# Placing the matmul operands of a three-block transformer at other bytes of SBUF

## The reference, cut to what matters

```python
def swiglu(h, w13, w2):
    a, b = jnp.split(h @ w13, 2, axis=-1)
    return (jax.nn.silu(a) * b) @ w2
...
        h = modulate(x, norm_g[l, 0], sh1, sc1)
        x = x + 0.5 * g1[:, None] * swiglu(h, ff_w13[l, 0], ff_w2[l, 0])
...
def moe_swiglu(h, w_router, w_gate, w_up, w_down):
...
    def expert_block(args):
        xb, e = args
        return swiglu_2(xb, w_gate[e], w_up[e], w_down[e])
```

## Time and profile before

| | |
|---|---|
| three runs | 3090.5 us median, 3087.42 to 3091.05 |
| span of the profiled execution | 3083.6 us |
| PE | busy 2999.6 us (97%), 20659 matmuls |
| DVE, ACT | busy 76% and 56% of the span |
| granted TensorE clock | 0.9 of full speed or more in each of the page's 40 slices |
| DMA | 240 GB/s in the mean |

### The profile page before, as it was taken

One profiled execution on the slowest core, in us unless ns is written; L12 is line 12 of the kernel. 1 busy time (PEld: TensorE's weight loads), 2 busy tenths in 40 slices (PEclk: granted clock), 3 DMA queues, 4 the chain that ended last, 5 costly groups with the idle time before them and its releaser, 6 DMA issues.

```text
span 3083.6 us, 48420 instructions
## 1 busy us (share of the span) xinstructions
PE 2999.6 (97%) x20659; PEld 2751.1 (89%) x20659; DVE 2343.1 (76%) x2704; ACT 1725.0 (56%) x1982; POOL 73.7 (2%) x143
## 2 busy tenths in 40 slices
PE   9999999999989999899989999999999999999999
PEld 8999899999979998899987888888888888899999
DVE  6887788888657566665777898898898898766675
ACT  5435443534535445444655777777777777555553
POOL 0110001010000000000000000000000000000000
PEclk9999999999999999999999999999999999999999
DMA  8785468587513543255415998998999899533353
GB/s 335 283 317 195 163 245 302 212 308 258 199 69 142 215 162 138 76 192 191 148 64 209 364 358 334 365 355 333 365 356 366 333 359 366 213 124 137 123 201 114
DMA packets 112381, 739.27 MB, mean 240 GB/s; under 512 B 12480, under 2 KB 12480, under 8 KB 32160
## 3 DMA queue, kind: packets, MB, share of 16 engines
q1 hardware_dynamic: 92304, 662.77, 57.3%
q0 software_dynamic: 19856, 73.34, 6.8%
HBM read 735.01 MB, written 1.05 MB: 239 GB/s over the span
## 4 chain that ended last, share of the span: by engine, by line
PE 86%; DVE 9%; ACT 3%; issue 1%; DMA 0%; SPq 0%; DVEq 0%; ACTq 0%
PE ps L560 65%; PE ps L559 19%; PE ps L569 2%; DVE wlo L2983 2%; ACT whi L1986 2%; DVE AF L2962 1%; DVE att L2971 1%; DVE T L2953 1%; DVE hl L2953 1%; DVE gf L2965 0%; ACT cv L1971 0%; DMA ring<-in_r 0%; DVE cv L2962 0%; DVE T L2962 0%; DVE AR L2962 0%
## 5 line engine op out<-in xcount | busy, mean ns | idle before, releaser
L2983 DVE TENSOR_TENSOR wlo<-ring,whi 128x2048 fp32r<-128x2048 f32 x620 | 1416.3, 2290 | 399.0 <-ACT whi L1986 398.3
L1986 ACT ACTIVATE whi<-ring 128x2048 fp32r<-128x2048 f32 x620 | 1184.4, 1914 | 310.6 <-issue 199.0
L560 PE MATMUL ps<-whi,AR 128*128 128x512 f32 (+1 forms) x2884 | 910.7, 392 | 0.3 <-DVE AF L2953 0.3
L560 PE MATMUL ps<-hh,whi 128*128 128x256 f32 x2272 | 641.8, 282 | 0.4 <-DVE hl L2953 0.4
L560 PEld LDWEIGHTS ps<-whi,AR 128*128 128x128 f32 x2884 | 535.5, 188 | 115.3 <-DVE AF L2953 0.7
L560 PE MATMUL ps<-hl,whi 128*128 128x256 f32 x2272 | 634.4, 279 | 0.0
L560 PE MATMUL ps<-hh,wlo 128*128 128x256 f32 x2272 | 634.3, 279 | 0.0
L560 PE MATMUL ps<-wlo,AR 128*128 128x512 f32 (+1 forms) x1442 | 557.4, 387 | 0.0
L560 PEld LDWEIGHTS ps<-hh,whi 128*128 128x128 f32 x2272 | 426.2, 188 | 5.8 <-issue 1.5
L560 PEld LDWEIGHTS ps<-hl,whi 128*128 128x128 f32 x2272 | 426.1, 188 | 1.2 <-issue 1.0
L560 PEld LDWEIGHTS ps<-hh,wlo 128*128 128x128 f32 x2272 | 425.9, 187 | 0.3
(11 more groups left out here) (275 smaller groups left out, 3481.6 us busy)
## 6 DMA issues: line engine op xcount, KB each, us to landing
ring<-in_w SPq DMA_DIRECT2D x620, 1024.0 KB, 4.9
rring<-in_r POOLq DMA_DIRECT2D x135, 512.0 KB, 5.0
first<-in_r SPq DMA_DIRECT2D x8, 512.0 KB, 18.4
ring<-in_r SPq DMA_DIRECT2D x4, 512.0 KB, 8.6
rring<-in_r SPq DMA_DIRECT2D x3, 512.0 KB, 17.4
AF<-in_mem SPq DMA_DIRECT2D x1, 1024.0 KB, 8.2
X<-in_x SPq DMA_DIRECT2D x1, 1024.0 KB, 16.2
AF<-in_cst POOLq DMA_DIRECT2D x1, 1024.0 KB, 5.3
```

The costliest lines, as they stand in the source:

```text
L560: return self.e.matmul(out, l, r, start=start, stop=stop)
L1986: self.e.activation(N.whi[:, c % HB, :], N.ring[:, c % RING, :], ACT.Copy).then_inc(N.sem["hi"], 1)
L2983: self.e.tensor_tensor(N.wlo[:, c % HB, :], N.ring[:, c % RING, :], N.whi[:, c % HB, :].bitcast(F32), ALU.subtract).then_inc(N.sem["lo"], 1)
```

## The change

No instruction is added, taken away or moved: on every engine the two programs have the same rows in the same order with the same waits. What changes is the byte at which some operands begin. The tiles `ca` and `gain` change places around `hh` and `hl`, a tile `gap` of 160 bytes that nothing uses stands ahead of `AR`, `AF` and `T`, and the unshifted early halves get a place of their own with a pitch of 256 numbers (`vh` and `vl`, picked by a new function `early_halves`).

The table has the first byte of each operand in its partition, as what is left of it over a multiple of 256. It follows from the sizes of the tiles: `X` begins at byte 16512, `ring` and the tiles up to `misci` stay where they were, and `AR` begins at byte 179488 before and 179648 now.

| operand | before | now |
|---|---|---|
| `whi`, `wlo` (every 128 or 512 columns of them) | 128 | 128 |
| `hh`, `hl`, each row | 160 | 64 |
| `f_gh`, `f_gl`, each row | 160 | 64 |
| unshifted early halves | 32, 64, 96, ... 0 for k = 0 to 7 | 64 in each row |
| shifted early halves | 32, 64, 96, ... 0 for k = 0 to 7 | 192, 224, 0, ... 160 |
| experts' `e_zeh`, `e_zel`, `e_gh`, `e_gl` | 32 | 192 |
| other tiles in `AR`, `AF` and `T` | 32 and others | 160 bytes on |

```diff
         self.X = sb("X", [P, 8, S])
-        self.ca = sb("ca", [P, 8])
+        self.gain = sb("gain", [P, 2, 3, 8])
         self.hh = sb("hh", [P, 8, S], F32R)
         self.hl = sb("hl", [P, 8, S], F32R)
-        self.gain = sb("gain", [P, 2, 3, 8])
+        self.ca = sb("ca", [P, 8])
         self.g12 = sb("g12", [P, 8])
...
         self.misci = sb("misci", [1, 8], I32)
+        self.gap = sb("gap", [P, 40])
         with nc.sbuf_tensor("AR", [P, 12288], F32R) as a:
             self.AR = a
...
         ar.n = 3840
         self.uh, self.ul = ar.take(8, UP), ar.take(8, UP)
         assert ar.n <= self.AF.shape[1] - 8 * S
+        ar = Arena(self.AR)
+        ar.n = 3872
+        self.vh, self.vl = ar.take(8, S), ar.take(8, S)
+        assert ar.n <= self.AF.shape[1] - 8 * S
...
+def early_halves(net, key):
+
+    return (net.uh, net.ul) if EARLY[key][0] == "mod" else (net.vh, net.vl)
...
         n = S + 2 if EARLY[h][0] == "mod" else S
+        uh, ul = early_halves(N, h)
...
-                    t = self.mm3(b[j][:, 0:n], whi[:, o:o + P], wlo[:, o:o + P], N.uh[:, k, 0:n], N.ul[:, k, 0:n],
+                    t = self.mm3(b[j][:, 0:n], whi[:, o:o + P], wlo[:, o:o + P], uh[:, k, 0:n], ul[:, k, 0:n],
                                  k == 0, k == 7)
```

More of the change, by code:

```diff
@@ L2095, in early @@
         gain, shift = gain_of(N, which)
+        uh, _ = early_halves(N, key)
         if self.loaded:
@@ L2104, in early @@
                 self.ready_x(j)
-                self.act(N.uh[:, j, 0:S], N.X[:, j, :], ACT.Copy, (key, "uhi", j), scale=gain[:, j:j + 1])
+                self.act(uh[:, j, 0:S], N.X[:, j, :], ACT.Copy, (key, "uhi", j), scale=gain[:, j:j + 1])
             if k == 0 and shift is not None:
-                self.act(N.uh[:, :, S:S + 2], shift.unsqueeze(2).to_broadcast([P, 8, 2]), ACT.Copy, (key, "ush"))
+                self.act(uh[:, :, S:S + 2], shift.unsqueeze(2).to_broadcast([P, 8, 2]), ACT.Copy, (key, "ush"))
             self.act(N.T[:, k:k + 2, :], N.X[:, k:k + 2, :], ACT.Square, (key, "sq", k), (key, "sq", k + 1))
@@ L3147, in early_after @@
         gain, shift = gain_of(N, EARLY[key])
+        uh, ul = early_halves(N, key)
         def rest(k):
@@ L3151, in rest @@
                 self.wait_ge("act", (key, "ush"))
-                self.tt(N.ul[:, :, S:S + 2], shift.unsqueeze(2).to_broadcast([P, 8, 2]), N.uh[:, :, S:S + 2].bitcast(F32),
+                self.tt(ul[:, :, S:S + 2], shift.unsqueeze(2).to_broadcast([P, 8, 2]), uh[:, :, S:S + 2].bitcast(F32),
                         ALU.subtract)
             self.wait_ge("act", (key, "uhi", k))
-            self.stt(N.ul[:, k, 0:S], N.X[:, k, :], gain[:, k:k + 1], N.uh[:, k, 0:S].bitcast(F32), ALU.mult, ALU.subtract,
+            self.stt(ul[:, k, 0:S], N.X[:, k, :], gain[:, k:k + 1], uh[:, k, 0:S].bitcast(F32), ALU.mult, ALU.subtract,
                      (key, "un", k))
```

## The result

The changed kernel takes 3067.1 us (median of four runs, 3060.5 to 3071.7) where the kernel before takes 3089.0 in the same comparison: a ratio of 0.9928, interval [0.9913, 0.9944]. It is faster by 22 us, 0.7%, where 75 us were forecast; the time lies 0.1 us past the end of the range.

A forecast was written before the change was run, and what follows sets the result against it. PE's matmul pace was taken as the bound; gains of 31.5 + 40.4 + 3 = 75 us off the 3083.6 us span give 3008.6, and 6.9 us from span to median gives 3015.5 us, range 2994 to 3067.

The forecast's parts named there:

- The rest: Unshifted early halves and some 670 further 256-column matmuls were to gain 3 us together; other engines' work was to stay unchanged.
- split x and gated halves: 11,664 matmuls of 256 columns, moved from byte 160 to 64, were to go from 116.7 to 113.7 ns: 31.5 us.
- The worst bound that I worked out: Smallest gain for the split x and gated halves: 115 ns per matmul, 19.8 us.
- The factor of 0.9: Share of the 256-column matmuls' 35.0 us gain taken to reach the end of the span, giving 31.5 us.
- the place makes no difference: Reading of memory products at byte 32 (120 ns) and 258-column halves at bytes 64 and 96 (120.8 ns and 1.44 us per 12).
- experts: 4038 matmuls of 512 columns, stationary moved from byte 32 to 192, were to go from 233.3 to 223.3 ns: 40.4 us.
- The first rival: The experts don't respond, perhaps because the moving operand's own byte, 64, counts: 3056 us, chance 0.20.
- it could fetch earlier: In the experts, the weights' queue waits 794.6 of 900 us for a freed buffer, so weights could keep up at 381 GB/s.
- the fourth rival: DMA or DVE holds PE up in the experts, and half of the 40.4 us stays: 3036 us, chance 0.10.
- Slower: Runs of `hh` and the gated halves settle at 120 ns and lose 35 us: 3125 us, chance 0.06.
- no change: The nine matmuls at 113.3 ns owe their pace to rows ahead; runs return to 116.7: 3090.5 us, chance 0.06.
- the forecast's own range: Times expected if the experts' matmuls take 220 to 226.7 ns: 2994 to 3040 us; the forecast's chance was 0.58.

The follow-up runs named there:

- experiment 3: Not the reference's work: 72 matmul streams alone, one per pair of start bytes, 256 or 512 columns; 113.3 to 120.0 ns per matmul at 256 columns, 226.7 to 234.4 at 512.
- experiment 4: Not the reference's work: 48 streams alone of 96 matmuls of 256 columns at bytes 64 and 128, 40 with an odd 49th matmul; 113.3 or 117.8 ns per matmul.
- experiments 5 to 7: The changed kernel with experts' stationary operands at byte 128 (3047.8 us), at byte 64 (3053.4 us), and at byte 128 plus 31 extra 254-column matmuls (3055.1 us).
- experiment 1: The changed kernel with the experts' stationary operands put back to byte 32, all else kept: 3065.5 us, ratio 0.9923 to the kernel before.
- experiment 5: The changed kernel with the experts' stationary operands at byte 128, the byte of their moving weights, instead of 192: 3047.8 us, ratio 0.9867 to the kernel before.
- experiment 8: The kernel of experiment 5 with only the first half of each expert weight chunk's columns fetched: 3047.4 us, ratio 0.9874 to the kernel before.

## Why the prediction was right and wrong

**Right: the place changes the pace of a matmul, and PE's pace is the time.** DVE, ACT and the 258-column halves (120.3 ns in the mean before, 120.2 now) stayed as they were. "The rest", 3 us, came out near its size: the unshifted early halves went from 117.7 to 115.1 ns (1.0 us), the matmuls with a weight as the moving operand from 118.9 to 116.7 (1.5 us). The Trainium skill, "SBUF — State Buffer", section "Who interferes with whom", calls PE's two read ports independent; by that rule experiment 3 would show one pace for all pairs, and it shows 113.3 to 120.0 ns with nothing else running.

**Wrong, step "split x and gated halves": "PE settles ... on a pace" and "a run of 48 matmuls or more now keeps it".** The nine matmuls of the earlier trace rows showed one of two stable states at that difference of bytes. A run does keep its state, but about a third of the matmuls are in the other one, at 117.8 ns. The term was 113.7 ns and 31.5 us; measured are 114.85 ns and 22.4 us of PE's work. The worst bound that I worked out, 115 ns, was the better guess. The factor of 0.9 is not what failed: 22 us of time for 25 us of PE's work (22.4 and 2.5 of the rest) do not speak against it.

The trace of the kernel before already had the sign. Its memory products, all at bytes 32 and 128, ran 15 matmuls in 1.80 us from 19 us on the earlier trace rows, but 12 us later in 33.37 - 31.61 = 1.76, 117.3 ns each, like k = 0 of the earlier trace rows at the same bytes:

```profile
31.61 0.28 PE L560 MATMUL ps<-AR,wlo 128*128 128x256 f32 x1
...
33.37 0.28 PE L560 MATMUL ps<-AR,wlo 128*128 128x256 f32 x1
```

Two paces at one pair of bytes, 120.0 and 117.3, were read as "the place makes no difference". Experiments 3 and 4 show both states of the pair 64 and 128 without any other work; what chooses between them inside the kernel is open: the second block's feed-forward had the better state in all eight profiled executions with operands at 64 and 128, the last one in three of eight (experiments 5 to 7).

**Wrong, step "experts": "so again the moving operand lies 64 bytes below the stationary one".** The good difference at 256 columns is not the good one at 512. There it is 0, which at 256 columns is among the worst (120.0 ns, and k = 3 of the earlier trace rows). The step carried a price from one shape to another with no row of the second; 40.4 us became nothing, as experiment 1 shows. The first rival had the outcome, with a wrong reason: it is not the moving operand's own byte, since 128 and 192 give 113.3 ns with 256 columns.

**Wrong, though it decided nothing: "it could fetch earlier".** I read the queue's 794.6 us of waiting as room. It is the opposite: the queue waits for a buffer of the ring, so the ring is in use all the time, and a chunk cannot be asked for sooner. Once PE was faster (experiment 5; experiment 8 takes the transfer's lateness away) the transfer became what is late, and the fourth rival, a part given back, came true there with 3 to 10 us.

**The rivals that fell.** Slower (pace at 120) and no change both fell on the interval of the result, [0.9913, 0.9944]. The range's end was meant as the first rival with the worst bound of the 256-column term, and near it the time came out, since that rival's outcome and nearly that bound's size came true. Its arithmetic slipped: 3090.5 - (17.8 + 3) is 3069.7, and what the rest can lose puts it later; 3067 takes the loss as a further gain. The end of the forecast's own range, 3040, has the same slip (3090.5 - 17.8 - 26.7 - 3 = 3043). Two smaller readings were off without consequence: one group of the earlier trace rows had waited 9.5 us, more than "a few", and six of the 4038 matmuls of 512 columns lie outside the experts (8 x 14 x 36 = 4032).

## What to carry to other kernels

When TensorE's streams are the bound, measure the pace of each shape for the start bytes it can have, in streams alone, and choose the difference per shape: here 64 at 256 columns of float32r and 0 at 512, 1.3% together (experiment 5) where the change as written has 0.7%. A pace seen in a few matmuls may be one of two states, so count intervals over the whole kernel, and repeat an execution before a stage's time is believed. A queue that waits most of the time for a buffer has no reserve, it is the ring's length that is used up; ask for the round trip of one buffer against the rate at which the work takes it.

## What was not expected of the hardware

- Matmuls of float32r with 256 columns at equal bytes run at 120.0 ns, at 64 bytes' difference at 113.3 or 117.8; with 512 columns they run at 226.7 and 233.4. Pairs with the same difference of start bytes over 256 have the same pace, or one of two (experiment 3).
- Two paces are stable at the same operands, and one matmul with 6 columns fewer can turn one into the other (experiment 4: seven of eight streams changed).
- A wait of 2.2 us in the changed kernel and one of 3.05 us in experiment 5 were each followed by seven matmuls of 512 columns at the 1.2 GHz level (427 ns); one of 2.82 us in experiment 5 was not.
